# Reordered boundaries of a two-layer encoder step: earlier rounding of inputs, earlier additions of one pair of tiles, and turns amid the last product

## What is computed

```python
def attn_mixer(h, w_in, q_w, k_w, past_k, past_v):
    qa, ka, va, g = jnp.split(h @ w_in, N_PROJ, axis=-1)
    q = rms_norm(qa.reshape(bn, t, N_HEADS, HEAD_DIM), q_w)
    k = rms_norm(ka.reshape(bn, t, N_HEADS, HEAD_DIM), k_w)
    ...
    o = stick_breaking(q, kk, vv, off).reshape(bn, t, D_MODEL)
    return o * jax.nn.silu(g), k, v

def hgrn_mixer(h, w_in, lb, out_w, S0):
    qa, fa, ia, g = jnp.split(h @ w_in, N_PROJ, axis=-1)
    ...
    o, S = hgrn2(heads(jax.nn.silu(qa)), heads(kk), heads(ia), heads(logf), S0)
    o = rms_norm(o, out_w).reshape(bn, t, D_MODEL).astype(h.dtype)
    return o * jax.nn.silu(g), S

    for layer in range(DEPTH):
        hp = rms_norm(xp, norm_w[layer])
        hs = rms_norm(xs, norm_w[layer])
        ...
        xp = xp + op @ w_out[layer]
        xs = xs + osm @ w_out[layer]
```

## Time and profile before

| | |
|---|---|
| three timed runs, median (lowest to highest) | 2231.52 us (2231.3 to 2231.74) |
| the profiled execution's own time | 2228.77 us |
| its span, first to last instruction | 2227.0 us |
| PE, weight loads, DVE, ACT busy | 2187.8, 2165.4, 1679.9, 1176.9 us |
| mean granted clock of PE | 0.997 |

### The profile page before, as it was taken

One profiled execution on the slowest core, in us unless ns is written; L12 is line 12 of the kernel. 1 busy time (PEld: TensorE's weight loads), 2 busy tenths in 40 slices (PEclk: granted clock), 3 DMA queues, 4 the chain that ended last, 5 costly groups with the idle time before them and its releaser, 6 DMA issues.

```text
span 2227.0 us, 41339 instructions
## 1 busy us (share of the span) xinstructions
PE 2187.8 (98%) x17137; PEld 2165.4 (97%) x17137; DVE 1679.9 (75%) x2788; ACT 1176.9 (53%) x1614; POOL 27.6 (1%) x46
## 2 busy tenths in 40 slices
PE   8999999999999999999999999999999999999899
PEld 7999999999999999999999999999999999999898
DVE  6888888888888888422467777777777777777676
ACT  6766666666656666422445544545444444545343
POOL 0000000000000000101000000000000000000000
PEclk9999999999999999999999999999999999999999
DMA  7433333333333336444422222222222222223453
GB/s 257 146 96 96 97 107 106 112 104 98 99 99 105 108 97 196 119 128 127 126 86 76 85 85 76 85 80 81 79 78 79 80 85 81 79 66 122 116 174 89
DMA packets 398432, 234.08 MB, mean 105 GB/s; under 512 B 9811, under 2 KB 379014, under 8 KB 398214
## 3 DMA queue, kind: packets, MB, share of 16 engines
q1 hardware_dynamic: 346198, 193.73, 30.2%
q10 hardware_dynamic: 52048, 37.71, 5.2%
HBM read 198.94 MB, written 32.46 MB: 104 GB/s over the span
## 4 chain that ended last, share of the span: by engine, by line
PE 91%; DVE 3%; ACT 3%; issue 1%; DMA 1%; ACTq 0%; SPq 0%; DVEq 0%
PE psum L737 44%; PE psum L945 28%; PE psum L1142 5%; PE psum L861 3%; PE psum L721 2%; ACT work L1172 1%; PE psum L836 1%; PE psum L784 1%; PE psum L810 1%; ACT act_hi L1172 1%; PE psum L820 1%; PE psum L907 1%; PE psum L886 1%; PE psum L909 0%; DVE w_lo L1700 0%
## 5 line engine op out<-in xcount | busy, mean ns | idle before, releaser
L737 PE MATMUL psum<-act_hi,w_hi 128*128 128x272 f32 x2876 | 609.3, 293 | 13.7 <-DVE work L2400 7.7
L737 PE MATMUL psum<-act_lo,w_hi 128*128 128x272 f32 x2876 | 594.9, 288 | 0.0
L737 PE MATMUL psum<-act_hi,w_lo 128*128 128x272 f32 x2860 | 593.1, 289 | 0.0
L1172 ACT ACTIVATE w_hi<-w_raw 128x1024 fp32r<-128x1024 f32 x356 | 372.7, 1056 | 403.2 <-PE psum L737 162.5
L737 PEld LDWEIGHTS psum<-act_hi,w_hi 128*128 128x128 f32 x2876 | 452.4, 189 | 15.8 <-issue 10.1
L737 PEld LDWEIGHTS psum<-act_lo,w_hi 128*128 128x128 f32 x2876 | 453.1, 189 | 0.0
L737 PEld LDWEIGHTS psum<-act_hi,w_lo 128*128 128x128 f32 x2860 | 448.7, 189 | 0.0
L1700 DVE TENSOR_TENSOR w_lo<-w_raw,w_hi 128x1024 fp32r<-128x1024 f32 x179 | 223.5, 1249 | 235.3 <-ACT w_hi L1172 234.8
L1172 ACT ACTIVATE work<-work 128x544 f32<-128x544 f32 (+6 forms) x336 | 235.1, 732 | 267.3 <-DVE work L1953 178.0
L945 PE MATMUL psum<-act_hi,w_hi 128*128 128x272 f32 x960 | 278.7, 290 | 1.8 <-DVE w_lo L1706 1.0
L945 PE MATMUL psum<-act_hi,w_lo 128*128 128x272 f32 x960 | 276.9, 288 | 0.0
(11 more groups left out here) (337 smaller groups left out, 3595.2 us busy)
## 6 DMA issues: line engine op xcount, KB each, us to landing
w_raw<-in_w_in SPq DMA_DIRECT2D x241, 512.0 KB, 4.1
w_raw<-in_w_out SPq DMA_DIRECT2D x62, 512.0 KB, 6.5
out<-work ACTq DMA_DIRECT2D x48, 256.0 KB, 4.4
x_residual<-work ACTq DMA_DIRECT2D x32, 272.0 KB, 3.8
work<-x_residual SPq DMA_DIRECT2D x32, 272.0 KB, 3.5
w_chain<-in_w_in SPq DMA_DIRECT2D x15, 512.0 KB, 4.3
full<-x_residual SPq DMA_DIRECT2D x8, 544.0 KB, 7.4
o_spill<-work ACTq DMA_DIRECT2D x15, 272.0 KB, 2.1
```

The source lines that it names most:

```text
L737: mm = pe.matmul(acc[par][:, j, :], at, a[:, k, j * HT:(j + 1) * HT], start=(k == 0 and n == 0), stop=(k == last and n == 2))
L1172: return nc.scalar.activation(out, in_, f, **kw)
```

## The change

It moves work; almost nothing is added. (A) At the end of layer 0's heads, rows 0 to 3 are rounded after the last product but one instead of the last, ahead of the weights of half tile g0 + 2, on ACT and on DVE. (B) At the end of layer 0's output projection, rows 0 to 7 are rounded and subtracted when the first two half tiles of the last pair are done, not after all four. (C) In the last HGRN head `lo(g0+3)` goes from behind step 1 to behind step 2, `hi(g0+4)` and `lo(g0+4)` from step 3 to step 4. (D) `NEXT_FILL` is 6 instead of 4. (E) The second plain pair's two additions go from the ends of steps 2 and 3 to the starts of steps 1 and 2 in DVE's queue, ahead of the weights' subtraction of that step; in the pairs by seven products the residual of one quarter is added to a partial sum instead of to the result. (F) The rows of the last but one tile to be stored are turned amid the last product, with the first two blocks of the last one; the last tile is copied and stored in two parts.

```diff
-NEXT_FILL = 4
+NEXT_FILL = 6
...
-                sp_eng.wait_ge(y_stored[par], 32 * (KT // 2))
+                sp_eng.wait_ge(y_stored[par], 32 * (KT // 2) + 16 * (1 - par))
...
-            def out_product(q, idx):
+            def out_product(q, idx, between=None):
...
-                    pe.wait_ge(fast_added, before + (1, 6, 5, 8)[idx])
+                    pe.wait_ge(fast_added, before + (1, 6, 5, 9)[idx])
...
+                    if between is not None and k == KH // 2:
+                        between()
                 mm.then_inc(half_done, 1)
+
+            def turn_last_rows():
+
+                turn_fast(FAST - 1, 1)
+                for b in range(2):
+                    mm = turn(M[2][:, b * P:(b + 1) * P], x_new[0][:, b * P:(b + 1) * P])
+                mm.then_inc(y_turned, 1)
+
+            def turn_last_half():
+                pe.wait_ge(fast_added, ADDED_IN + OUT_EVACS * FAST)
+                for b in range(2, NB):
+                    turn(M[3][:, (b - 2) * P:(b - 1) * P], x_new[0][:, b * P:(b + 1) * P])
+                turn(M[3][:, 2 * P:3 * P], x_new[0][:, LAST:T]).then_inc(y_turned, 1)
...
             for q in range(FAST):
                 for idx in range(PRODUCTS):
-                    out_product(q, idx)
+                    out_product(q, idx, turn_last_rows if (q, idx) == (FAST - 1, PRODUCTS - 1) else None)
...
-            turn_fast(FAST - 1, 1)
-            turn_fast(FAST - 1, 0)
+            turn_last_half()
...
                 if l == 1:
 
+                    act.wait_ge(half_done, LAYER_BASE[1])
                     act.wait_ge(full_ready, KT)
-                    act_split(range(2, KT))
+                    act_split(range(KH, KT))
...
                 for u in range(-1, 7):
                     if u == -1:
                         if l == 0:
-                            hi(g0 + 2, 2)
-                        if l == 0:
-                            act.wait_ge(half_done, g0)
+                            act.wait_ge(half_done, g0 - 1)
...
-                    if l == 1 and u == 0:
+                    if u == 1 - l:
                         act.wait_ge(half_done, g0)
                     elif l == 1 and u == 3:
                         act.wait_ge(o_ready, H + H - 1)
                     act_split(LAST_SPLIT[l][u], l == 0)
+                    if l == 0 and u == -1:
+                        hi(g0 + 2, 2)
                     if u == 1:
                         hi(g0 + 3, 3)
-                    if u == 4 - l:
+                    if u == 4:
                         hi(g0 + 4, 0)
...
+                        if l == 0 and last and u == 2:
+
+                            act.wait_ge(half_done, LAYER_BASE[1] - 2)
+                            act.wait_ge(full_ready, KH)
+                            act_split(range(KH))
                         if l == 0 and u >= 2:
-                            out_tile(i, u - 2, last)
+                            out_tile(i, u - 2)
...
-                    if last and par:
-
-                        act.wait_ge(half_done, LAYER_BASE[1])
-                        act.wait_ge(full_ready, 2)
-                        act_split(range(0, 2))
...
             put_fast(FAST - 1, 1)
-            put_fast(FAST - 1, 0)
+            for part_ in range(2):
+                blocks = slice(2 * part_, 2 * part_ + 2)
+                cols = slice((KT - 2) * P, (KT - 1) * P)
+                act.wait_ge(y_turned, KT + part_)
+                act.wait_ge(y_stored[0], 32 * (KT // 2 - 1))
+                ins = func(y_nat[0][:, blocks, :], M[2 + part_][:, 0:2 * P].rearrange(
+                    "p (b d) -> p b d", b=2), ACT.Copy)
+                ch.done(ins)
+                if part_:
+                    func(y_nat[0][:, 4, :], M[3][:, 2 * P:3 * P], ACT.Copy).then_inc(y_copied, 1)
+                ch.wait()
+                act.dma_start(y_prompt_v[:, blocks, cols], y_nat[0][:, blocks, :]).then_inc(y_stored[0], 16)
+            act.wait_ge(y_copied, KT)
+            act.dma_start(y_sample[0][:, cols], y_nat[0][SROW:P, 4, :]).then_inc(y_stored[0], 16)
...
                 if l == 1:
-                    act_split(2 * KT, range(KT))
+                    act_split(2 * KT, range(KH, KT))
...
-                        if u == -1:
-                            lo(g0 + 2, 2)
                     elif u >= 0:
                         rec_dve(H - 1, u)
                     if l == 0 and u in LAST_LOW:
                         act_split(KT, LAST_LOW[u])
+                        if u == -1:
+                            lo(g0 + 2, 2)
                     if l == 1 and u == 4:
                         act_split(3 * KT, [KT - 2])
-                    if u == 1:
+                    if u == 1 + l:
                         lo(g0 + 3, 3)
-                    if u == 4 - l:
+                    if u == 4:
                         lo(g0 + 4, 0)
...
                             lo(i * 4 + (OUT_BASE[l] + u + AHEAD), (u + AHEAD) % RING)
+                        if last:
+                            act_split(2 * KT, range(KH // 2 * par, KH // 2 * (par + 1)))
...
                     put(x_new[1][:, 0:HT], x_new[1][:, 0:HT], x_old[1][:, 0:HT])
+                    put(out_u2, out_u2, x_old[0][:, HT:T])
                 else:
+                    dve.wait_ge(fast_added, base + 8)
                     put(x_new[0][:, HT:T], z, out_u2)
-                    dve.wait_ge(fast_added, base + 8)
-                    put(x_new[0][:, HT:T], x_new[0][:, HT:T], x_old[0][:, HT:T])
...
             for i in range(1, PLAIN):
                 for u in range(4):
+                    if i == 1 and u in (1, 2):
+                        plain_added(1, u - 1)
...
-                    if u >= 2:
+                    if i > 1 and u >= 2:
                         plain_added(i, u - 2)
```

More of the change, by code:

```diff
@@ L1582, in out_pair, with out_tile @@
                             hi(i * 4 + (OUT_BASE[l] + u + AHEAD), (u + AHEAD) % RING)
+                        if l == 0 and last and u == 2:
+                            act.wait_ge(half_done, LAYER_BASE[1] - 2)
+                            act.wait_ge(full_ready, KH)
+                            act_split(range(KH))
                         if l == 0 and u >= 2:
-                            out_tile(i, u - 2, last)
+                            out_tile(i, u - 2)
                         if l == 1 and u < 2 and not first:
                             put_y(i - 1, u)
-                def out_tile(i, par, last):
+                def out_tile(i, par):
                     n = i * 2 + par
-                    if last and par:
-                        act.wait_ge(half_done, LAYER_BASE[1])
-                        act.wait_ge(full_ready, 2)
-                        act_split(range(0, 2))
                     act.wait_ge(evacuated, added(l, n))
```

## The result

The changed kernel takes **2218.28 us** (median of 5 runs, 2217.51 to 2218.69) against 2231.3 us for the kernel before beside it (2227.45 to 2231.74): a ratio of 0.9945, with an interval of 0.9934 to 0.9956, or some 12 to 13 us. The profiled execution took 2217.51 with a span of 2215.8; spans fell by 11.2.

A forecast was written before the change was run, and what follows sets the result against it. TensorE was taken as the bound, so only its waits could pay. A to F sum to 9.5 us: the span of 2227.0 becomes 2217.5, the profiled execution 2219.3, and with 2.75 added 2222.0; range 2219.4 to 2225.2.

The forecast's parts named there:

- A: Layer 0's last attention head: the first act_lo wait goes, L784's wait grows by what was saved; 0.25 us left.
- B: Turn to layer 1: the act_lo waits of 2.7 us go and nothing becomes late; 2.7 us, bounds 2.0 to 2.8.
- C: Last HGRN head: own_lo's wait goes, but only the second moved subtraction brings L861 forward; 1.2 us, bounds 0.6 to 2.6.
- D: Wait before L1089: twelve matmuls move into it, a small new weight wait takes part; 1.3 us, bounds 1.0 to 1.5.
- E: Second plain pair: the 7.7-us addition wait becomes about 4.3 us for ACT's copy; 3.65 plus 0.05 us, bounds 2.0 to 4.5.
- F: Tail: ACT's first copy starts 1.1 us earlier, the split store costs 0.75; 0.35 us saved, bounds -0.3 to 0.6.
- The timed runs lie 2.75 above it: Sum: timed median 2231.52 against the profiled execution's 2228.77 us; this 2.75 us was added to the new time.
- The clock rival: Second plain pair: clock falls in the 4.3-us wait left, costing 0.05 to 0.5 us; 2222.1 to 2222.5; chance 0.25.
- A wait of about 2 before the second product: Expected sign of E in the plain pairs: PE waits about 2 us for the differences before the second product.
- Slower: Second plain pair: the moved addition waits for late residual rows, differences come 10.4 us later; 2238.6 us; chance 0.03.
- E nothing: Second plain pair: a load or another handshake holds the differences, ACT's idle time is not recovered; 2225.7 us; chance 0.12.
- B nothing: Turn to layer 1: the half-way wait holds ACT and rounding still comes last, no gain; 2224.7 us; chance 0.04.

The follow-up runs named there:

- c1: Kernel before with only the last HGRN head's two weight subtractions and one rounding moved later; 2227.09 us, ratio 0.9983.
- c2: Kernel before with spare matmuls in the last HGRN head's two waits, the second group standing behind the wait and lengthening it; 2231.85 us, ratio 1.0004.
- e4: Changed kernel with 36 spare matmuls in the 5-us wait ahead of the second plain pair's second turns; 2218.9 us, 0.9949 of the kernel before.
- e3: Kernel before with 56 spare matmuls ahead of the plain pair half tile that waits 7.7 us for the addition; 2229.93 us, ratio 0.9996.
- e1: Changed kernel with the second plain pair's two additions put back in their old place; 2223.17 us, 0.9968 of the kernel before.
- f1: Changed kernel with turns still amid the last product, but the last tile turned, copied and stored whole; one execution, span 2218.1 us.
- f2: Changed kernel with the tail's turns back behind the last product and the last tile whole, still one addition there; one execution, span 2217.2 us.
- e2: Kernel before with only the second plain pair's two additions moved forward; 2226.32 us, ratio 0.9980.
- e5: Changed kernel with the first two plain pairs' output store issues moved from ACT to SyncE; 2214.86 us, 0.9931 of the kernel before.
- e7: Changed kernel with a row's four differences ahead of the same step's weight subtraction on VectorE; 2212.86 us, 0.9924 of the kernel before.

## Why the prediction was right or wrong

**A** (0.25): right. A and B together are 3.4 (first column of the marks); L784 comes 0.15 to 0.2 earlier, and its wait grew from 0.5 to 1.7 as the in-order queue of ACT demanded.

**B** (2.7, at most 2.8): the mechanism right, the size 0.5 too small. No wait for `act_lo` is left at the turn. A wait's row gives the time from the modelled end of the matmul ahead to the next start; without a wait the next one starts 0.16 before that end (L737 ends at 1098.70 and L1017 starts at 1098.54 in the changed kernel). The two waits of 2.7 in all were thus worth 3.0 to 3.1, of 3.2 measured. The last 0.1 to 0.2 is open.

**C** (1.2; bounds 0.6 to 2.6): the mechanism right, the size wrong. The profile to profile difference is 1.20, as worked out, with L861's wait at 1.6 and `own_lo`'s gone. But the time of the kernel fell by 3.8 with C alone. What the working lacked is the load behind ACT's rounding and the clock behind the wait: 952.70 is one execution's value, 954.9 and 954.6 those of two others.

**The step that failed** is therefore in the sum: "The timed runs lie 2.75 above it", taken as a constant and added to the new time. c1's 3.8 less the 1.2 of the profiled execution makes 2.6 us that the timed runs lose in the head, by the traces to late weights and the clock, a place which the change itself clears up; for the changed kernel the timed median lies only 0.8 above the profiled execution. With 2.6 taken off, the forecast of 2222.0 becomes 2219.4; B's 0.5 and F's 0.9 more, D's and E's 1.1 less, make it 2219.1. The last 0.8 is within what the start does (its first mark was 51.7 in the changed kernel, 53.2 in the one before, 52.4 on average over the traces) and what the clock behind E's old wait adds in other executions, 0.46 on average over the five traces and 1.25 in c2, which the change also removes. c1's own interval leaves 0.6 to 4.6 for the 2.6. The row that could have warned was in the trace: the moved rounding waits 0.16 for its DMA, so it was level with its load, and a wait of PE stood right behind it.

**D** (1.3) **and E** (3.7): 5.0 forecast, 3.94 measured in the changed kernel, 4.45 in e4 (counted from the profiled execution of before, where the 48 matmuls behind E's wait took 7.76; c2 has 9.01). The wait of 4.3 for ACT's copy came as forecast, as 5.05, and 0.8 of the shortfall is one row: the second store's issue took 1.35 instead of the 0.53 that it had before, in the chain; with 0.53, e4's chain would end at 54.26, and the forecast was 54.2. It was 1.05 to 1.64 in every trace with E whose stores stood on ACT. SyncE's next load is issued at that very moment (2068.31), because the freed additions let it go earlier; but in e3, without E, it took 1.26 with no issue of SyncE beside it, so the cause stays open. D's 1.3 was 1.07 up to the next turn in the changed kernel and 1.08 up to E's wait in e1, where the longer fall of the clock took it away again.

**The clock rival** (chance 0.25, price 0.05 to 0.5) held: the clock fell 3.1 us after PE stopped. What it cost beyond the slack is the stretch less e4's 54.78, corrected for the issue: 0.2 in the changed kernel, 0.7 in f1 and 0.3 in f2 (where the issue took 1.59 and 1.19). "A wait of about 2 before the second product" didn't appear for that reason, and in e4, without the fall, it did (1.77). The Trainium skill, page "TensorE: Matmul & The Clock Gate", section "HAM oscillation — how this bites in real kernels", has it that long waits send the array back to half clock each time; here it did so behind the waits of 2.41 (e2), 2.79 (c2), 2.98 (e5), 5.05 (changed) and 7.75 us (before), so the trace agrees. What the rule doesn't weigh is what binds behind the wait: at 7.75 the price, 1.5 and more, reached product 1 in full, and at 5.05 the chain of ACT and DVE hid all but 0.2.

**F** (0.35; bounds -0.3 to 0.6): 1.2 measured, the forecast too small. The first copy starts 1.13 earlier behind product 1's turn, as worked out, and the last issue ends 0.74 earlier: the added copy and issue cost 0.39, not 0.75. And the execution ends 0.5 sooner after that issue, a term that the sum did not have.

**Slower, E nothing, B nothing**: none occurred. The late residual rows did not matter.

## What to carry to other kernels

Before a difference between a profiled execution and the median is carried over as a constant, ask which place of the program makes it, and whether the change removes that place: an instruction that is level with its load (a wait for a DMA of 0.1 or 0.2 us in front of it) is late in other executions, and the median contains it. An engine behind which work piles up is shortened by what stands in its queue without being its work: the issue of a store (0.9 to 2 us for two) on a chain of rounding and subtraction is worth as much as the arithmetic. Work that has its operands should stand ahead of work that waits for another engine, as the four differences in e7, worth some 5 us. And what a fall of the clock costs is set by what binds behind it: the same kind of fall was paid in full before the change and nearly hidden after it.

## What the runs showed of the hardware

- The clock can fall after the wait is over: in e5 PE had been idle for 2.98 us and was busy again from 2082.53, and the clock fell some 1 us later; in e3 some 1.3 us after L861 had started behind a wait of 1.96. It was back 3.3 us after PE's restart in the kernel before and 4.9 us after it in the changed one, and behind the same wait of 7.7 the 48 matmuls took 7.56 to 9.01 us in five executions (6.26 at full clock, e3). Behind L861's waits of 1.58 to 1.68 it did not fall in any of ten traces.
- The issue of a 16 KB store on ACT took 0.53 or 1.05 to 1.64 us in the same place of the program.
- The end of the execution came 1.83 us after the last 16 KB store's issue where the large store just ahead of it was 128 KB, and 2.3 where it was 256 KB.
